# Modulation products in column groups of the PE array, and the narrow projection turned round, in a trunk layer with two token mixers

## The reference, cut to what matters

```python
def adaln(cvec, w, b):
    return jax.nn.silu(cvec) @ w + b            # 2 x 1024 by 1024 x 6144
...
sh_a, sc_a, gt_a, sh_f, sc_f, gt_f = jnp.split(mod[:, None, :], N_MOD, axis=-1)
h = rms_norm(x, lp['g_mix_pre']) * (1.0 + sc_a) + sh_a
proj = h @ lp['w_in']
z, xbc, dt_raw, q, k, v, o, gate_raw, merge_raw = jnp.split(
    proj, np.cumsum(IN_SPLITS)[:-1].tolist(), axis=-1)
```

## Time and profile before

| | |
|---|---|
| median of 3 executions | 2923.81 us (2922.86 to 2925.49) |
| the profiled execution | 2928.07 us |
| its span | 2926.4 us |
| PE busy | 2565.0 us, 88% of the span |
| DVE, ACT, POOL busy | 1525.8, 906.5, 799.4 us |
| channel tiles (L484), PE | 512 records, 226.4 us busy, 0.0 us idle before them |
| later modulation products (L516), PE | 128 records, 16 for each of 8 chunks |
| mean DMA rate over the span | 320 GB/s |

### The profile page before, as it was taken

One profiled execution on the slowest core, in us unless ns is written; L12 is line 12 of the kernel. 1 busy time (PEld: TensorE's weight loads), 2 busy tenths in 40 slices (PEclk: granted clock), 3 DMA queues, 4 the chain that ended last, 5 costly groups with the idle time before them and its releaser, 6 DMA issues.

```text
span 2926.4 us, 26223 instructions
## 1 busy us (share of the span) xinstructions
PE 2565.0 (88%) x8280; PEld 1324.8 (45%) x8280; DVE 1525.8 (52%) x3674; ACT 906.5 (31%) x2428; POOL 799.4 (27%) x705
## 2 busy tenths in 40 slices
PE   7999999899967879989988899799899988888876
PEld 3555555444323644445544355444455443443332
DVE  1330022111011875569865678755698657666674
ACT  2110111000021443255532454432545334343332
POOL 0011100000000233344333333333443324444453
PEclk8999999999978999999999999999999999999999
DMA  5133324444346699999999999999999999999996
GB/s 213 49 111 110 118 84 159 176 159 168 115 156 229 268 425 426 427 418 411 377 426 427 426 416 360 425 426 426 420 408 380 426 427 426 412 427 426 424 418 290
DMA packets 138038, 937.70 MB, mean 320 GB/s; under 512 B 16503, under 2 KB 20855, under 8 KB 35241
## 3 DMA queue, kind: packets, MB, share of 16 engines
q0 software_dynamic: 98720, 694.73, 57.0%
q1 hardware_dynamic: 33562, 200.40, 17.9%
q10 hardware_dynamic: 5616, 40.90, 3.4%
HBM read 898.16 MB, written 37.81 MB: 320 GB/s over the span
## 4 chain that ended last, share of the span: by engine, by line
DMA 28%; PE 24%; DVE 8%; ACT 4%; DVEq 2%; issue 2%; POOL 1%; ACTq 0%; SPq 0%; POOLq 0%
DMA e_expert<-in_peer_uv,e_idx 27%; PE e_acc L1548 15%; DVE e_expert L1666 3%; PE e_qs L1563 3%; PE e_B L1481 2%; DVEq L1668 1%; ACT e_diag L1434 1%; POOL e_expert L1345 1%; PE e_A L1481 1%; ACT e_coef L1429 1%; PE e_A L849 0%; DMA e_wb<-in_w_out 0%; ACT e_act L1426 0%; ACT e_mg L909 0%; ACTq L1430 0%
## 5 line engine op out<-in xcount | busy, mean ns | idle before, releaser
L1548 PE MATMUL e_acc<-e_expert,e_diag 128*128 128x512 f32 x2560 | 1206.1, 618 | 236.0 <-ACT e_diag L1434 235.6
L1345 POOL DMA_INDIRECT e_expert<-in_peer_uv,e_idx x640 | 757.2, 1183 | 1294.0 <-PE e_acc L1548 1110.7
L1666 DVE CUSTOM_DVE_ANT_0 e_expert<-e_expert,e_xb 128x1024 f32<-128x1024 f32 x640 | 777.1, 1224 | 495.1 <-DMA e_expert<-in_peer_uv,e_idx 466.3
L1548 PEld LDWEIGHTS e_acc<-e_expert,e_diag 128*128 128x128 f32 x2560 | 484.2, 197 | 872.2 <-issue 515.4
L514 PE MATMUL pj<-w_chunk,hT 128*128 128x512 f32 x800 | 357.5, 605 | 9.5 <-DMA w_chunk<-in_w_big 7.3
L1426 ACT ACTIVATE e_act<-e_dots 128x2 f32<-128x2 f32 x320 | 65.0, 203 | 850.9 <-DVEq L1668 849.4
L514 PEld LDWEIGHTS pj<-w_chunk,hT 128*128 128x128 f32 x800 | 154.0, 195 | 196.4 <-issue 193.4
L1434 ACT ACTIVATE e_diag<-ident,e_coef 128x128 f32<-128x128 f32 x640 | 221.9, 394 | 22.3 <-issue 0.4
L484 PE MATMUL pj<-hT,w_chunk 128*128 128x512 f32 x512 | 226.4, 595 | 0.0
L1429 ACT ACTIVATE e_coef<-e_act,e_gate 128x1 f32<-128x1 f32 x640 | 154.0, 287 | 23.0 <-issue 1.1
L1563 PEld LDWEIGHTS e_qs<-e_h2T,e_w_head 128*128 128x128 f32 x1280 | 148.0, 192 | 9.8 <-issue 9.6
(11 more groups left out here) (369 smaller groups left out, 2139.2 us busy)
## 6 DMA issues: line engine op xcount, KB each, us to landing
e_wb<-in_w_out SPq DMA_DIRECT2D x60, 1024.0 KB
e_w_head<-in_w_q ACTq DMA_DIRECT2D x39, 1024.0 KB
w_chunk<-in_w_big SPq DMA_DIRECT2D x18, 2048.0 KB, 9.0
w_chunk<-in_w_mod SPq DMA_DIRECT2D x8, 2048.0 KB, 9.1
scratch_proj<-tile_out POOLq DMA_DIRECT2D x10, 1280.0 KB
e_expert<-in_peer_uv,e_idx POOLq DMA_INDIRECT x640
wm<-in_w_mod SPq DMA_DIRECT2D x4, 2048.0 KB, 20.5
e_m<-scratch_mod_rows SPq DMA_DIRECT2D x15, 512.0 KB, 7.5
```

The costliest lines, as they stand in the source:

```text
L1345: nc.gpsimd.indirect_dma_start(expert[:, u % RING, :], None, dr["peer_uv"], bass.IndirectOffsetOnAxis(idx[:, h % 4, s:s + 1], 0)).then_inc ...
L1548: mm = nc.tensor.matmul(acc[:, c * 512:(c + 1) * 512], diag[:, (u + j) % RING, :], expert[:, (u + j) % RING, D + c * 512:D + (c + 1) * 512 ...
L1666: nc.vector.tensor_tensor_reduce(expert[:, u % RING, 0:D], expert[:, u % RING, 0:D], xb[p % 2][:, :], 1.0, 0.0, ALU.mult, ALU.add, dots[:, ...
```

## The change

It edits phases 1 and 2:

- `cv` becomes 32 columns wide, 30 of them zero. A modulation chunk's 8 products go in turn to three groups of 32 columns of the array (`row_parts`), each group gathering its own sum in 32 of 96 PSUM rows. DVE copies the 96 rows to SBUF, and a further product with a 0/1 tile (`pick`) sums the three groups. In phase 1 this product has the copied rows as its loaded side, so that the result comes out as columns, 4 products for each chunk; bias and gain are then added on columns by DVE. In phase 2 `pick` is the loaded side and one product of 512 columns gives the two rows.
- In phase 1 the scaling of `hT` is split 3 to 5 between ACT and DVE, not 4 to 4.
- The narrow projection has its weights (padded to 64 columns) as the loaded side and the tokens streaming, in two groups of 64 columns; ACT copies the sums to `smallT`, and 5 products with `pick` behind the first channel tile add the two groups and turn them back.
- The narrow weights, the convolution parameters and the first two weight chunks of phase 2 are loaded by SP at the end of phase 1's list, into tiles and on semaphores of an outer context.
- In phase 2, PE runs the summing product of a mod unit behind the unit that follows it, DVE's copy takes the place that `mod_result` had, and `mod_result` comes one unit later.

```diff
@@ new, above modulate_and_normalise
+MOD_M, MOD_ROWS, SMALL_M = 32, 96, 64
...
+def row_parts(nc, to, cv, w):
+    for k in range(KT):
+        g = k % 3
+        last = nc.tensor.matmul(to[MOD_M * g:MOD_M * (g + 1), :], cv[:, k, :], w[:, k, :], start=(k < 3), stop=(k >= KT - 3))
+    return last
@@ modulate_and_normalise, SP
-            sp.dma_start(bias[:, :], dr["b_mod"][:, 0:2 * D].partition_broadcast(2)).then_inc(small_in, 16)
-            sp.dma_start(gain[:, :], dr["gain_rows"][:, 0:D].partition_broadcast(2)).then_inc(small_in, 16)
+            sp.dma_start(bias[:, :, :], dr["b_cols"]).then_inc(small_in, 16)
+            sp.dma_start(t["gains"][:, :, :], dr["gains"]).then_inc(small_in, 16)
...
-            sp.dma_start(t["gains"][:, :, :], dr["gains"]).then_inc(later_in, 16)
             sp.dma_start(t["rows"][:, :], dr["small_rows"].partition_broadcast(P)).then_inc(later_in, 16)
-            sp.wait_ge(later_in, 32)
+            sp.dma_start(ahead["ws"][:, :, :], dr["w_small"]).then_inc(ahead["par_in"], 16)
+            sp.dma_start(ahead["cw"][:, :, :], dr["convT"]).then_inc(ahead["par_in"], 16)
+            for n in range(2):
+                sp.dma_start(ahead["w"][:, n], dr["w_big"][STREAM[n][1]]).then_inc(ahead["w_in"][n], 16)
+            sp.wait_ge(later_in, 16)
@@ modulate_and_normalise, PE
+            def columns(n):
+                v, half = n // 2, 4 * (n % 2)
+                pe.wait_ge(part_ready, n + 1)
+                for i in range(4):
+                    last = nc.tensor.matmul(col_ps[:, v, half + i, :], parts[:, n % 2, i * P:(i + 1) * P], t["pick"][0:MOD_ROWS, 48:50],
+                                            start=True, stop=True)
+                last.then_inc(cols_summed, 1)
...
+            pe.wait_ge(picks_ready, 1)
+            for n in range(MOD_FIRST // 2):
+                columns(n)
             for n in range(MOD_FIRST // 2, MOD_FIRST):
                 chunk(n)
-            pe.wait_ge(vec_ready, MOD_FIRST)
-            for v in (V_SCALE_A, V_SHIFT_A):
-                for k in range(KT):
-                    last = nc.tensor.transpose(col_ps[:, v, k, :], vec[:, v, k * P:(k + 1) * P], t["ident"][0:2, 0:2])
-            last.then_inc(cols_turned, 1)
+            for n in range(MOD_FIRST // 2, MOD_FIRST):
+                columns(n)
@@ modulate_and_normalise, DVE
+            def part(n):
+                dve.wait_ge(chunk_mm, n + 1)
+                if n >= 2:
+                    dve.wait_ge(cols_summed, n - 1)
+                nc.vector.tensor_copy(parts[:, n % 2, :], row_ps[n % 2][:, :]).then_inc(part_ready, 1)
+
+            dve.wait_ge(const_ready, CONSTANTS)
+            nc.vector.tensor_tensor(t["pick"][:, 0:48], t["ident"][:, 0:48], t["ident"][:, 64:112], ALU.add)
+            dve.drain()
+            nc.vector.tensor_tensor(t["pick"][:, 48:50], t["ident"][:, 32:34], t["pick"][:, 0:2], ALU.add)
...
+            dve.wait_ge(cols_summed, MOD_FIRST)
+            nc.vector.tensor_tensor(cols[:, :, :, :], col_ps[:, :, :, :], bc_last(bias[:, :, :], 2), ALU.add)
+            dve.drain()
+            nc.vector.scalar_tensor_tensor(cols[:, V_SCALE_A, :, :], cols[:, V_SCALE_A, :, :], 1.0, bc_last(t["gains"][:, 0, :], 2),
+                                           ALU.add, ALU.mult)
...
-            for k in range(KT // 2, KT):
+            for k in range(3, KT):
@@ project_and_scan, SP
-            sp.dma_start(ws[:, :, :], dr["w_small"]).then_inc(par_in, 16)
-            sp.dma_start(cw[:, :, :], dr["convT"]).then_inc(par_in, 16)
-            for n in range(X_CH + Q_CH + 1):
+            for n in range(2, X_CH + Q_CH + 1):
@@ project_and_scan, PE
-            for b in range(BLOCKS):
+            for bank, tokens in ((unit_bank[0], slice(0, 512)), (unit_bank[1][:, 0:P], slice(512, TOK))):
                 for k in range(KT):
-                    last = nc.tensor.matmul(unit_bank[0][:, b * 48:(b + 1) * 48], hT[:, k, b * P:(b + 1) * P], ws[:, k, :],
-                                            start=(k == 0), stop=(k == KT - 1))
-            last.then_inc(small_mm, 1)
+                    g = SMALL_M * (k % 2)
+                    last = nc.tensor.matmul(bank[g:g + SMALL_M, :], ws[:, k, :], hT[:, k, tokens], start=(k < 2), stop=(k >= KT - 2))
+                last.then_inc(small_parts, 1)
+
+            def small_columns():
+                pe.wait_ge(small_out, 2)
+                for b in range(BLOCKS):
+                    last = nc.tensor.matmul(unit_bank[2][:, b * 48:(b + 1) * 48], smallT[:, b * P:(b + 1) * P], t["pick"][:, 0:48], start=True, stop=True)
+                last.then_inc(small_mm, 1)
...
+                if n == 0:
+                    small_columns()
...
+                    last = row_parts(nc, to, t["cv"], w[:, n % 2])
                 last.then_inc(unit_mm, 1)
+                if k and units[k - 1][1] == "mod":
+                    row_sum(k - 1)
...
+            def row_sum(k):
+                pe.wait_ge(part_ready, units[k][2] + 1)
+                nc.tensor.matmul(unit_bank[k % 3][0:2, :], t["pick"][0:MOD_ROWS, 48:50], parts[:, :], start=True, stop=True).then_inc(row_mm, 1)
@@ project_and_scan, DVE
+            def mod_part(k):
+                at, kind, i, b = units[k]
+                if kind != "mod":
+                    return
+                dve.wait_ge(unit_mm, k + 1)
+                if i:
+                    dve.wait_ge(row_mm, i)
+                nc.vector.tensor_copy(parts[:, :], unit_bank[k % 3][0:MOD_ROWS, :]).then_inc(part_ready, 1)
...
-                    mod_result(k - 1)
+                    mod_part(k - 1)
+                    if k >= 2:
+                        mod_result(k - 2)
```

More of the change, by code:

```diff
@@ L102, in modulate_and_normalise @@
         sem = semaphores(nc, ctx)
-        cv, sig = t["cv"], sb("cv_sig", [P, KT, 2])
+        cv, sig = t["cv"], sb("cv_sig", [P, KT, MOD_M])
         wm = sb("wm", [P, MOD_FIRST, KT, 512])
-        bias, gain = sb("mod_bias", [2, 2 * D]), sb("mod_gain", [2, D])
-        raw, vec = sb("mod_raw", [2, 2, 512]), sb("mod_vec", [2, 2, D])
+        bias = sb("mod_bias", [P, 2, KT])
+        parts = sb("mod_parts", [MOD_ROWS, 2, 512])
         cols = sb("mod_cols", [P, 2, KT, 2])
@@ L153, in _ @@
                 nc.scalar.copy(hT[:, 4 * half:4 * half + 4, b * P:(b + 1) * P], ps[n % 4][:, :, :]).then_inc(moved, 1)
-            act.wait_ge(cols_turned, 1)
-            nc.scalar.copy(cols[:, :, :, :], col_ps[:, :, :, :])
             act.drain()
-            act.sem_inc(cols_ready, 1)
-            for k in range(KT // 2):
+            act.wait_ge(cols_ready, 1)
+            for k in range(3):
                 for c, tokens in enumerate((slice(0, P), slice(P, TOK))):
@@ L197, in _ @@
             nc.vector.tensor_tensor(cv[:, :, :], cv[:, :, :], sig[:, :, :], ALU.mult).then_inc(silu_ready, 1)
-            def vector(n):
-                v, w = n // 2, slice((n % 2) * 512, (n % 2) * 512 + 512)
+            def part(n):
                 dve.wait_ge(chunk_mm, n + 1)
[L203 to L210, removed]
+                if n >= 2:
[6 more added lines that the diff above has]
+            dve.drain()
+            dve.sem_inc(picks_ready, 1)
+            part(0)
             dve.wait_ge(sums_ready, 1)
@@ L347, in project_and_scan @@
         sem = semaphores(nc, ctx)
-        w = sb("w_chunk", [P, 2, KT, 512])
-        ws = sb("w_small", [P, KT, 48])
-        cw = sb("conv_par", [P, 4, 16])
+        w, ws, cw = ahead["w"], ahead["ws"], ahead["cw"]
+        smallT = sb("small_turned", [P, TOK])
+        parts = sb("row_parts", [MOD_ROWS, 512])
         acc = sb("conv_acc", [P, 2, TOK])
@@ L1784, in programme @@
         t["small"], t["gates"] = sb("small", [P, BLOCKS, 48]), sb("gates", [P, BLOCKS, G_N])
-        t["cv"] = sb("cv", [P, KT, 2])
-        with nc.sbuf_tensor("hT", [P, KT, TOK], F32) as hT:
-            modulate_and_normalise(nc, dr, t, hT)
-            project_and_scan(nc, dr, t, hT)
+        t["cv"], t["pick"] = sb("cv", [P, KT, MOD_M]), sb("pick", [P, 50])
+        with ExitStack() as first:
+            held = lambda n, s: first.enter_context(nc.sbuf_tensor(n, s, F32))
+            sem = semaphores(nc, first, "ahead_")
+            hT = held("hT", [P, KT, TOK])
+            ahead = {"w": held("w_chunk", [P, 2, KT, 512]), "ws": held("w_small", [P, KT, SMALL_M]), "cw": held("conv_par", [P, 4, 16]),
+                     "w_in": [sem("w_in0"), sem("w_in1")], "par_in": sem("par_in")}
+            modulate_and_normalise(nc, dr, t, hT, ahead)
+            project_and_scan(nc, dr, t, hT, ahead)
         experts(nc, dr, t)
@@ L1826, in layout @@
     out["w_big"] = tiles(cat(z, v, o, m, xbc, q, k))
-    out["w_small"] = tiles(cat(dt, g), 48)[0]
+    out["w_small"] = tiles(cat(dt, g, np.zeros((D, SMALL_M - 48), np.float32)), SMALL_M)[0]
     out["convT"] = cols(cat(i["conv_w"][0], i["conv_b"], axis=0))
```

49 lines of the change are left out of this document (29 added, 20 removed).

## The result

The changed kernel took **2929.45 us** (median of 20 runs, 2922.98 to 2936.26) against 2922.85 for the kernel before (20 runs, 2919.64 to 2930.30): a ratio of **1.0022, 95% interval 1.0015 to 1.0029**. Faster was predicted; it is slower, by little, but measurably.

The account below looks back on a forecast made before the run. PE was taken to bound the opening stage, weight loads the later chunks, gathers a fixed tail. Terms -5.8, -2.5, +0.5, -10.1, -1.4, +1.2, +4.0 sum to -14.1 us: 2910 us, range 2899 to 2920.

Parts of the forecast that it names:

- fixed tail: Expert gathers and products behind the last stored row: unedited, so gains or losses in front reach the end one for one.
- three at a time: Rival: three column-group products overlap fully, 2.58 us a chunk; -19.6 us in all, ending at 2904; chance 0.27.
- the one that ended slower, at 2934: Rival: column groups don't overlap and weight loads aren't hidden, a chunk taking more than 7 us; chance 0.07.
- Chunk price: Modulation chunk in three column groups: 3.87 us, between 2.58 with three at a time and 6.87 without overlap.
- Opening stage: Phase 1 up to the end of the hT scaling: ends at 48.1 us against 53.9, 5.8 us gained.
- Stage boundary: Between hT scaling and narrow projection: PE starts about 0.9 us after the scaling, not 3.4; 2.5 us gained.
- narrow projection: Start of phase 2 on PE: 17.1 us become 7.0, the first 4.0 us at half clock; 10.1 us gained.
- first tile: First channel tile: PE's clock is already up, so 16 records take 7.03 us, not 8.41; 1.4 us gained.
- turning back: Five products behind the first channel tile that turn the narrow result back: 10 records, 1.2 us lost.
- The eight later chunks: Phase 2 modulation chunks: shorter products lengthen DMA waits, with cold starts and summing products added; 4.0 us lost.
- the barrier: End of the projection phase: one more clearing of semaphores and barrier, 0 to 0.9 us, taken as 0.5 lost.
- the last row stored near 850: Sign at the end of phase 2: SP's last row store, at 851.25 us before, would stay near 850.

Follow-up runs that it names:

- a1: The changed kernel with the pick tile widened from 50 to 80 columns, putting the expert ring back on a multiple of 256 bytes; 2906.63 us, ratio to before 0.9944.
- b1: The kernel before with an unused 40-column tile behind cv, so the expert ring starts 160 bytes past a multiple of 256; 2947.47 us, ratio 1.0081.
- a5: a1 with only the expert ring moved to 160 bytes past a multiple of 256, other tiles in place modulo 256; 2930.19 us, ratio 1.0020.
- c2: a1 with a chunk's products in group order 0,0,0,1,1,1,2,2 instead of in turn; 2909.18 us, a single execution.

## Why the prediction was wrong

**The step that failed** is the first: "the change edits nothing in it, so I take it as a fixed tail". Nothing was edited, but the tail is bound by the gathers, and the wider `cv` and the `pick` tile moved their target. It grew by 22.3 us. a1 takes that move back, b1 makes it without the change, and a5 confines it to the ring: 23 us each time, to within one (2929.45 - 2906.63, 2947.47 - 2924.16, 2930.19 - 2906.63). In all nine kernels with the ring on a multiple of 256 the tail is 2066 to 2075 us, in all five others 2093 to 2103. Without this, the forecast would have been near: a1, the change with the ring in place, took 2906.63, inside the range. That is 17.5 us below its kernel before, between the 14.1 of the forecast and the 19.6 of the rival "three at a time". No rival had the tail; the one that ended slower, at 2934, did so because the groups don't overlap, and that the measured time lies near it is chance.

**Chunk price.** 3.87 us was taken; it is 2.77, near the lower bound of 2.58. The term was mis-sized by 1.1 us a chunk. PE's weight loads in chunk 6 show three products at a time: three load records start in each of these slots of 0.43 us, in which one record started before.

```profile
777.62 0.12 PEld L101 LDWEIGHTS pj<-w_chunk,cv 128*32 128x32 f32 x3 [0.31 <-issue]
778.04 0.12 PEld L101 LDWEIGHTS pj<-w_chunk,cv 128*32 128x32 f32 x3 [0.30 <-issue]
```

My argument that the second record of a product must hold up the next group was wrong: with the groups in turn, it doesn't. The rival "three at a time" had the front nearly right: -19.6 predicted by it, -19.3 measured in this pair of profiles. The Trainium skill (TensorE: Matmul & The Clock Gate, Part 3, "Measured speedup vs the span model") gives 2.38 times for three column tiles; here it is 6.87 / 2.77 = 2.5, so rule and trace roughly agree. The Trainium skill (TensorEngine Tiling (Array Packing), Key Properties) says that a change of the tiling mode drains the engine. These rows show no cost of it: the product behind chunk 0 starts 0.07 us before the chunk's last record ends (467.46 + 2.77 against 470.16 below), and it was 0.07 in the earlier trace rows, within one mode (21.09 + 7.03 against 28.05). The ends of PE's records are modelled in the profile, so this is the overlap of records, not a measured drain.

**Opening stage.** The scaling ends at 40.62 + 3.65 = 44.3 us: -9.7, where -5.8 was taken and three at a time gave -9.7. DVE's 3.65 and the summing products' 1.84 and 1.95 are as predicted. Chunk 1 came cold (at half clock), as predicted, but stayed so to its end: 5.34 us for 2.77, at a granted clock of 0.50 (windows below).

**Stage boundary, narrow projection, first tile, turning back.** PE starts 0.9 us behind the scaling: -2.5, right. The narrow projection takes 45.15 to 52.29, -10.0 for -10.1: right by two errors that cancel. Its products were faster than I took them, and the half clock lasted longer than 4 us: the granted clock was 0.50 from 45.1 to 49.4 and 0.79 from there to 52.3. So its 7.14 us are some 4.4 us of work at full clock (4.3 x 0.50 + 2.9 x 0.79), what both groups at once would take (8 x 0.43 + 8 x 0.12), and not the 5.0 that I took. Windows of the changed kernel: stretch, length, busy by engine, then PEclk:

```profile
21.20:26.60 5.40, 5.34 (x17) 1.02 (x18) 1.59 (x3) 0.00 (x0) 0.00 (x0) 0.50 1.02 434
45.10:49.40 4.30, 4.25 (x10) 1.37 (x12) 0.00 (x0) 0.00 (x0) 0.00 (x0) 0.50 0.00 0
49.40:52.30 2.90, 2.90 (x25) 1.50 (x21) 0.00 (x0) 0.59 (x1) 0.00 (x0) 0.79 0.00 0
```

The first tile's 7.13 us gives -1.3 and the five products +1.1, as predicted. In all, the first big unit starts at 330.42 instead of 352.69, -22.3; before, then after:

```profile
352.69 7.03 PE L514 MATMUL pj<-w_chunk,hT 128*128 128x512 f32 x16
```

```profile
330.42 7.03 PE L547 MATMUL pj<-w_chunk,hT 128*128 128x512 f32 x16
```

**The eight later chunks.** PE's timeline, with the waits in brackets, against the earlier trace rows:

```profile
467.46 2.77 PE L101 MATMUL pj<-w_chunk,cv 128*32 128x512 f32 x16
470.16 2.87 PE L942 MATMUL pj<-s_v,s 128*128 128x257 f32 x12
474.42 7.11 PE L547 MATMUL pj<-w_chunk,hT 128*128 128x512 f32 x16 [1.38 <-DMA w_chunk<-in_w_big]
481.45 1.02 PE L560 MATMUL pj<-row_parts,pick 96*2 96x512 f32 x2
...
527.66 8.80 PE L547 MATMUL pj<-w_chunk,hT 128*128 128x512 f32 x16 [4.12 <-DMA w_chunk<-in_w_big]
...
581.07 9.80 PE L547 MATMUL pj<-w_chunk,hT 128*128 128x512 f32 x16 [5.31 <-DMA w_chunk<-in_w_big]
...
639.77 1.97 PE L821 MATMUL pj<-ident,s_turned 128*128 128x128 f32 x8 [12.40 <-DMA s_turned<-scratch_xbcT]
...
692.17 8.80 PE L547 MATMUL pj<-w_chunk,hT 128*128 128x512 f32 x16 [3.21 <-DMA w_chunk<-in_w_big]
...
739.55 9.07 PE L547 MATMUL pj<-w_chunk,hT 128*128 128x512 f32 x16 [7.27 <-DMA w_chunk<-in_w_big]
...
786.51 9.48 PE L547 MATMUL pj<-w_chunk,hT 128*128 128x512 f32 x16 [6.58 <-DMA w_chunk<-in_w_big]
...
824.53 2.77 PE L101 MATMUL pj<-w_chunk,cv 128*32 128x512 f32 x16
828.09 1.02 PE L560 MATMUL pj<-row_parts,pick 96*2 96x512 f32 x2 [0.79 <-DVE row_parts L653]
```

The mechanism is as predicted. The shorter product turns into a longer wait for what comes next, the weights behind six of the chunks and `s_turned` behind chunk 3 (12.40 us for 7.74), and 16 records behind a wait of 3.21 us or more for weights take 8.80 to 9.80 us instead of 7.0. The page has it in one row, after and then before: these units wait 27.9 us for w_chunk, against 7.3.

```profile
L547 PE MATMUL pj<-w_chunk,hT 128*128 128x512 f32 x800 | 364.0, 613 | 30.0 <-DMA w_chunk<-in_w_big 27.9
```

```profile
L514 PE MATMUL pj<-w_chunk,hT 128*128 128x512 f32 x800 | 357.5, 605 | 9.5 <-DMA w_chunk<-in_w_big 7.3
```

The summing product costs its 0.95 and waits for DVE only once, 0.79 us at the last chunk. From the first big unit to `e_w_head` it is 504.0 us against 501.1, +2.9; over all profiles of this study the new form takes 499.7 to 507.0 (seven, c2's other order left out, mean 504.0) and the old one 496.2 to 501.9 (six, mean 499.0), +5.0. Predicted were +4.0 and 0.5 for the barrier, +4.5: right, as far as profiles that spread over 6 to 7 us can tell. The end of the phase, where 0.5 was taken for the barrier, became 1.1 us longer: from the last row stored to `e_w_head` it is 834.46 - 830.82 = 3.64 us, and was 853.80 - 851.25 = 2.55.

**The sum.** Front -22.3 + 2.9 = -19.4, and the unedited phase +22.3: +2.9, and the spans differ by 3.0. One sign of the prediction didn't follow from its own sum: "the last row stored near 850" should have read 837 (851.25 - 14.1); it was stored at 830.82.

## What to carry to other kernels

A tile that grows or is added moves all tiles behind it, so "this phase isn't edited" is no proof that its time stays: where a phase is bound by gathers of long rows, keep their target on a multiple of 256 bytes of the partition, or place it ahead of the small tiles (not tried here). For plain loads no such loss was found: in b1 `w_chunk` lay 160 bytes past a multiple of 256 as well, and the stretch from the first big unit to `e_w_head` took 496.2 us, against 501.1 before. Column groups pay where PE's products set the end (phase 1, the narrow projection) and lose where the next load does: there the shorter product becomes a longer wait with a start at half clock behind it, and the summing product comes on top. Let consecutive products use different groups (0.9 us a chunk in c2).

## What the runs showed of the hardware that was not expected

The rate at which gathers of 8 KB rows fill SBUF depends on where the target begins: on a multiple of 256 bytes q0's packets took 1664 to 1672 us in nine kernels, 32, 128 or 160 bytes past one 1690 to 1695 in five, and the fullest slices fell from 426 or 427 GB/s to 420 to 422. The queue q1, with 200 MB of plain loads and stores, hardly differs by the same reckoning: 523 to 526 us in the nine kernels, 525 to 527 in the five. The Trainium skill (DMA: Bandwidth & Descriptors, "How a descriptor splits into AXI transactions") states that a transaction can read less than 256 bytes but must start at a 256-byte boundary, and that the bytes ahead of an unaligned start still cost beats. That is about what a descriptor reads; here it is the written side that moved. The step of 256 agrees. The size doesn't: by its count of beats applied to the written side, an estimate, an 8 KB row would take 0.4% more at 32 past, 1.6% at 128 and 2.0% at 160; measured were 1.6%, 1.3% and 1.3% against the 1668 of before.
